# Hybrid encoder trunk on one core: the first two SSD heads prepared during the input projection, `x*dt` built per pair of heads, one 128-row spread matmul, and the MLA operands built during the last heads

## The reference

```python
def ssd_scan(x, dt, a, b_in, c_in):        # run forwards, and on the flipped sequence
    def step(state, inp):                  # chunks of 128 tokens
        xc, dtc, bc, cc = inp
        acum = jnp.cumsum(dtc * a, axis=1)
        diff = acum[:, :, None] - acum[:, None, :]
        decay = jnp.exp(jnp.where(causal, diff, -jnp.inf))
        cb = jnp.einsum('blgn,bsgn->blsg', cc, bc)
        scores = cb[..., None] * decay * dtc[:, None]
        y = jnp.einsum('blsge,bsgep->blgep', scores, xc)
        ...
def ssd_mla_mixer(h, w_in, ...):
    proj = jnp.einsum('bsd,df->bsf', h, w_in)
    z, xbc, dt_raw, q_a, kv_a = jnp.split(proj, [o1, o2, o3, o4], axis=-1)
    xbc = jax.nn.silu(dwconv_centred(xbc, conv_w, conv_b))
    ...                                    # xs, b_in, c_in from xbc; dt = softplus(...)
    y = y_fwd + y_bwd + xs * d_skip
    y = rmsnorm(y * silu(z), ssd_norm_w)
    o_mla = mla_attention(q_a, kv_a, ...)
    return jnp.einsum('bsf,fd->bsd', jnp.concatenate([y, o_mla], axis=-1), w_out)
```

## Time and profile before

| | us |
|---|---|
| median of 3 runs | 1456.57 (1453.92 to 1461.63) |
| profiled execution, its own time | 1456.77 |
| its span in the trace | 1454.9 |
| TensorE busy | 1386.8 (95% of the span) |
| VectorE busy | 826.2 (57%) |
| ScalarE busy | 644.8 (44%) |
| GpSimd busy | 634.0 (44%) |

### The profile page before, as it was taken

One profiled execution on the slowest core, in us unless ns is written; L12 is line 12 of the kernel. 1 busy time (PEld: TensorE's weight loads), 2 busy tenths in 40 slices (PEclk: granted clock), 3 DMA queues, 4 the chain that ended last, 5 costly groups with the idle time before them and its releaser, 6 DMA issues.

```text
span 1454.9 us, 16724 instructions
## 1 busy us (share of the span) xinstructions
PE 1386.8 (95%) x6722; PEld 1142.5 (79%) x6722; DVE 826.2 (57%) x980; ACT 644.8 (44%) x983; POOL 634.0 (44%) x291
## 2 busy tenths in 40 slices
PE   6999798898999999999999999997999999999997
PEld 6778565677889888888888977886798888888886
DVE  5656487564007999888100755345158998885003
ACT  4544375554234544444223465534444544443221
POOL 2345485103541455444555244422714554545550
PEclk9999899999999999999999999998999999999998
DMA  5222100112322232322333312211113323323331
GB/s 186 85 87 87 36 1 1 37 42 75 91 84 91 97 101 89 101 91 91 94 101 89 114 58 87 90 42 44 65 52 116 100 88 102 92 93 95 93 92 58
DMA packets 36685, 117.76 MB, mean 81 GB/s; under 512 B 3840, under 2 KB 8320, under 8 KB 36608
## 3 DMA queue, kind: packets, MB, share of 16 engines
q1 hardware_dynamic: 35888, 114.63, 25.0%
q10 hardware_dynamic: 720, 2.06, 0.4%
HBM read 114.58 MB, written 2.10 MB: 80 GB/s over the span
## 4 chain that ended last, share of the span: by engine, by line
PE 75%; DVE 7%; ACT 3%; issue 1%; POOL 0%; DVEq 0%; ACTq 0%
PE bank L312 22%; PE bank L314 22%; PE bank L313 22%; PE bank L1134 2%; PE bank L1267 1%; PE bank L1268 1%; DVE ebuf L1010 1%; DVE ebuf L1003 1%; PE bank L1290 1%; DVE xres L559 1%; PE bank L402 1%; ACT prob L1339 1%; PE bank L1471 0%; DVE xw_lo L578 0%; DVE m_ffn L552 0%
## 5 line engine op out<-in xcount | busy, mean ns | idle before, releaser
L295 POOL TENSOR_TENSOR wlo<-raw,whi 128x1024 fp32r<-128x1024 f32 (+2 forms) x216 | 529.2, 2464 | 704.5 <-ACT whi L289 704.4
L312 PE MATMUL bank<-xw_hi,whi 128*128 128x512 f32 (+1 forms) x1360 | 516.0, 379 | 16.0 <-DVE xw_lo L578 11.9
L314 PE MATMUL bank<-xw_hi,wlo 128*128 128x512 f32 (+1 forms) x1360 | 505.4, 372 | 0.0
L313 PE MATMUL bank<-xw_lo,whi 128*128 128x512 f32 (+1 forms) x1360 | 505.2, 371 | 0.0
L289 ACT ACTIVATE whi<-raw 128x1024 fp32r<-128x1024 f32 (+2 forms) x217 | 220.7, 1023 | 223.2 <-DMA raw<-in_fout 113.4
L312 PEld LDWEIGHTS bank<-xw_hi,whi 128*128 128x128 f32 x1360 | 259.4, 191 | 67.5 <-issue 17.9
L313 PEld LDWEIGHTS bank<-xw_lo,whi 128*128 128x128 f32 x1360 | 259.4, 191 | 47.3 <-issue 3.6
L314 PEld LDWEIGHTS bank<-xw_hi,wlo 128*128 128x128 f32 x1360 | 259.0, 190 | 45.1
L531 DVE RECIPROCAL small<-small 128x2 f32<-128x2 f32 (+1 forms) x12 | 2.0, 170 | 353.0 <-ACT small L468 337.4
L635 DVE SCALAR_TENSOR_TENSOR cbuf<-ubuf,par,cbuf 128x510 f32<-128x510 f32 x100 | 170.8, 1708 | 3.5
L631 DVE SCALAR_TENSOR_TENSOR cbuf<-ubuf,par,cbuf 128x510 f32<-128x510 f32 x100 | 149.9, 1499 | 0.6 <-ACT cbuf L665 0.6
(11 more groups left out here) (252 smaller groups left out, 1465.0 us busy)
## 6 DMA issues: line engine op xcount, KB each, us to landing
raw<-in_fin SPq DMA_DIRECT2D x88, 512.0 KB, 3.6
raw<-in_fout SPq DMA_DIRECT2D x32, 448.0 KB, 3.3
raw<-in_gin SPq DMA_DIRECT2D x25, 512.0 KB, 3.5
raw<-in_hin SPq DMA_DIRECT2D x24, 512.0 KB, 3.6
raw<-in_hout SPq DMA_DIRECT2D x16, 512.0 KB, 3.6
raw<-in_fout SPq DMA_DIRECT2D x16, 512.0 KB, 3.5
raw<-in_gout SPq DMA_DIRECT2D x8, 512.0 KB, 3.6
xres<-in_x SPq DMA_DIRECT2D x8, 256.0 KB, 7.6
```

Source lines behind the costliest of these rows:

```text
L295: engine.tensor_tensor(wlo[s][:, 0:n], raw[s][:, 0:n], whi[s][:, 0:n].bitcast(F32), ALU.subtract).then_inc(w_lo, 1)
L312: first = nc.tensor.matmul(out_ap, wh, ah, start=start, stop=False)
L313: nc.tensor.matmul(out_ap, wh, al, start=False, stop=False)
L314: return first, nc.tensor.matmul(out_ap, wl, ah, start=False, stop=stop)
```

## The change

It does four things. (a) `pe_x_turn` stands after z blocks 17, 18, 19 and 20; the last four z blocks use banks 6 and 7; and heads 0 and 1 are spread after block 21, their exponentials, minima and masks standing between the last z blocks on each engine. (b) `xdt` is cut by pair of heads (128x512 for one direction of one pair, all four token blocks), pairs 0 and 1 are made ahead of the masks of head 0, pairs 2 and 3 after the last z block, pairs 4 to 7 by GpSimd behind the masks of heads 2 to 9. (c) High and low part of the cumulated sum lie on 128 rows of one tile, `at_both`, the low part brought there by a DMA from ScalarE's queue, so one matmul replaces two. (d) The rounded MLA operands and the two matmuls on `mq` stand before the end of the heads.

```diff
@@ pe_hin
-            return bank[(4, 5)[j] if j < 2 else j % 2 if j >= 20 else (0, 1, 3)[(j - 2) % 3]]
+            return bank[(4, 5)[j] if j < 2 else 7 - j % 2 if j >= 20 else (0, 1, 3)[(j - 2) % 3]]
...
-                if j >= 20:
-                    pe.wait_ge(sem("hin_u"), (18, 19, 21, 22)[j - 20])
-                elif j >= 5:
+                if j == 21:
+                    pe.wait_ge(sem("cb_set"), 16)
+                elif j >= 22:
+                    pe.wait_ge(sem("hin_u"), j - 1)
+                elif 5 <= j < 20:
                     pe.wait_ge(sem("hin_u"), j - 2)
...
-            for t in range(Z0, 12):
-                if t == 11:
+                if 0 <= j - TURN0 < NBLK:
+                    pe_x_turn(pe, j - TURN0)
+                if j == 21:
                     pe.wait_ge(sem("hin_u"), 20)
                     pe_spread(pe, 0, True)
-                block(2 * t)
-                block(2 * t + 1)
-                pe_x_turn(pe, t - Z0)
+                    pe_spread(pe, 1, True)
@@ act_hin
+            act.wait_ge(sem("dt_dve"), 9)
+            act.dma_start(at_both[64:128, :].bitcast(F32), at_lo[:].bitcast(F32)).then_inc(sem("at_in"), 16)
             turns(act, SIDE, Z0, conv)
...
+            for j in range(2 * Z0, 24):
+                gate(j)
+                i = j - TURN0
+                if 0 <= i < NBLK:
+                    act.wait_ge(sem("xs_T"), 2 * i + 1)
+                    nc.scalar.activation(xtok[0][:, i * T:(i + 1) * T], bank[4][:],
+                                         ACT.Copy).then_inc(sem("xtok_act"), 1)
+                if j == 21:
+                    act_exps(act, 0)
+                    act_exps(act, 1)
@@ dve_hin
+                if j == 20:
+                    dve.wait_ge(sem("xtok_act"), NBLK)
+                    dve.wait_ge(sem("dt_dve"), 12)
+                    dve_xdt(dve, 0)
+                    dve_xdt(dve, 1)
+                if j == 21:
+                    dve_least(dve, 0)
+                    dve_least(dve, 1)
+                    dve_mask(dve, 0)
+                if j == 22:
+                    dve_mask(dve, 1)
@@ pool_hin
-            for at in range(BASE["hin"], BASE["hin"] + 23):
+            for at in range(BASE["hin"], BASE["hin"] + 22):
                 los(pool, at)
+            pool.wait_ge(sem("cb_mm"), NBLK)
+            pool.wait_ge(sem("xtok_act"), NBLK)
+            pool.wait_ge(sem("dt_dve"), 12)
+            pool_xdt(pool, 0, 1)
+            pool_xdt(pool, 1, 1)
+            pool_mask(pool, 0)
+            pool_mask(pool, 1)
+            los(pool, BASE["hin"] + 22)
@@ xdt by pair of heads
+        def xdt_part(engine, d, p):
+            f0 = d * NBLK * P
+            dt = dtt[:].rearrange("p (b n) -> p b n", b=NBLK)[:, :, d * 32 + 2 * p:d * 32 + 2 * p + 2]
+            return engine.tensor_tensor(
+                xdt[p][:, f0:f0 + NBLK * P].rearrange("p (b h e) -> p b h e", b=NBLK, e=HDIM),
+                xtok[p // 4][:].rearrange("p (b q h e) -> p b q h e", b=NBLK, q=4, h=2)[:, :, p % 4],
+                dt.unsqueeze(3).broadcast_to([P, NBLK, 2, HDIM]), ALU.mult)
@@ pool_ssd
+            pool.wait_ge(mm, BASE["hin"] + 24)
+            pool_xdt(pool, 2, 1)
+            pool_xdt(pool, 3, 1)
+            pool.wait_ge(sem("xtok_dve"), NBLK)
+            for n in range(2, HEADS):
+                pool_mask(pool, n)
+                if n < 10:
+                    pool_xdt(pool, 4 + (n - 2) // 2, n % 2)
@@ dve_ssd
+            dve_xdt(dve, 2)
+            dve_xdt(dve, 3)
+            dve.wait_ge(sem("xdt_pool"), 4)
+            dve.wait_ge(sem("xdt_dve"), 4)
...
+            for n in range(HEADS):
+                if n + 2 < HEADS:
+                    dve_least(dve, n + 2)
+                if n >= 2:
+                    dve_mask(dve, n)
+                if n % 2 and n >= 3:
+                    gated((n - 3) // 2)
+            dve_mla_low(dve)
             gated(KD - 1)
@@ act_ssd
-            for n in range(HEADS):
-                exps(n, n % 4, n < 4)
+            for n in range(2, HEADS):
+                act_exps(act, n)
                 if n % 2 and n >= 5:
                     square((n - 5) // 2)
+            act_mla_prep(act)
@@ pe_spread
-                pick = ident_r[:, 32 * d + n:32 * d + n + 1].to_broadcast([64, P])
-                nc.tensor.matmul(abank(v, d)[:], pick, at_hi[:],
-                                 start=True, stop=False)
-                nc.tensor.matmul(abank(v, d)[:], pick, at_lo[:],
-                                 start=False, stop=True).then_inc(sem("a_mm"), 1)
+                pick = ident_r[:, 32 * d + n:32 * d + n + 1].to_broadcast([P, P])
+                nc.tensor.matmul(abank(v, d)[:], pick, at_both[:], start=True, stop=True).then_inc(sem("a_mm"), 1)
@@ pe_ssd
-            pe.wait_ge(sem("hin_u"), 24)
-            pe_spread(pe, 1, True)
             pe_spread(pe, 2)
-            pe.wait_ge(sem("xdt_dve"), NBLK)
-            pe.wait_ge(sem("xdt_pool"), NBLK)
...
+                if n == HEADS - 1:
+                    pe_mla_prep(pe)
                 y(n)
```

More of the change, by code:

```diff
@@ L139, in build_program @@
         with ExitStack() as s:
-            xdt = sb("xdt", 2 * NBLK * D, F32, s)
+            xdt = [None, None] + [sb(f"xdt{p}", 2 * NBLK * P, F32, s) for p in range(2, PAIRS * 2)]
         with ExitStack() as s:
@@ L156, in build_program @@
             with ExitStack() as q:
+                with ExitStack() as q2:
+                    sb("xs_chunks", 8 * T, F32, q2)
+                    xdt[0:2] = [sb(f"xdt{p}", 2 * NBLK * P, F32, q2) for p in range(2)]
                 xbc = sb("xbc", 12 * T, F32, q)
@@ L1026, in gated @@
                 nc.vector.tensor_tensor(ck(zbuf, c), ck(zbuf, c), ck(xbc, c), ALU.mult).then_inc(sem("ssd_y"), 1)
-            def turn(n0, g, first=False, last=False):
-                for v in range(4):
-                    if v < 2 or not last:
-                        least(n0 + v + 2, (v + 2) % 4, first and v < 2)
-                    m(n0 + v, v, g)
-                    if (n0 + v) % 2 and n0 + v >= 3:
-                        gated((n0 + v - 3) // 2)
-            turn(0, 0, first=True)
-            turn(4, 0)
-            turn(8, 1)
-            turn(12, 1, last=True)
+            for n in range(HEADS):
[6 more added lines that the diff above has]
+            dve_mla_low(dve)
             gated(KD - 1)
@@ new lines, in act_exps @@
+        def act_exps(act, n):
+            v = n % 4
+            act.wait_ge(sem("a_mm"), 2 * n + 2)
+            if n == 0:
+                act.wait_ge(sem("dt_dve"), 12)
+            if n == 2:
+                act.wait_ge(sem("xdt_pool"), 4)
+                act.wait_ge(sem("xdt_dve"), 4)
+            if n >= 4:
+                act.wait_ge(sem("y_mm"), n - 3)
+            for r, s, a, b, l0 in TILES[0]:
+                nc.scalar.activation(ebuf[v][:, r * 384 + a:r * 384 + b],
+                                     abank(v, 0)[:, r * SEQ + l0:r * SEQ + l0 + b - a], ACT.Relu, scale=-1.0,
+                                     bias=acol[:, bass.ds((2 * r + s) * 64 + n, 1)]).then_inc(
+                                         sem("ssd_rel"), 1)
+            act.wait_ge(sem("ssd_rel"), 4 * n + 4)
+            nc.scalar.activation(ebuf[v][:, 0:768], ebuf[v][:, 0:768], ACT.Exp, scale=-1.0).then_inc(
+                sem("ssd_exp"), 1)
+            act.wait_ge(sem("ssd_min"), 4 * n + 4)
+            nc.scalar.activation(ebuf[v][:, 768:1536], ebuf[v][:, 768:1536], ACT.Exp).then_inc(
+                sem("ssd_exp"), 1)
@@ L1200, in dve_mla_low @@
                 dve.wait_ge(sem("mla_hi"), i + 1)
-                nc.vector.scalar_tensor_tensor(out=dst, in0=ck(mq, 1 + i), scalar=w, in1=src.bitcast(F32),
+                nc.vector.scalar_tensor_tensor(out=dst, in0=ck(mq, 1 + (i + 1) % 3), scalar=w, in1=src.bitcast(F32),
                                                op0=ALU.mult, op1=ALU.subtract).then_inc(sem("mla_lo"), 1)
         def pe_mla_prep(pe):
-            pe.wait_ge(sem("ssd_y"), 16)
-            nc.tensor.matmul(bank[4][:], con("seldup"), ck(mq, 0), start=True, stop=True)
@@ L1951, in _ @@
             act_ssd(act)
-            act_mla_prep(act)
             act_mla(act)
@@ L1969, in _ @@
             pool_hin(pool)
-            pool_xdt(pool)
             pool_ssd(pool)
```

185 lines of the change are left out of this document (75 added, 110 removed).

## The result

The changed kernel takes 1441.84 us (median of 4 runs, 1441.08 to 1442.44), before 1459.1 in the same comparison. The two medians differ by 17.3 us; the ratio of the measurement is 0.9892, with a 95% interval of 0.987 to 0.9914, which is 15.8 us less. The profiled execution took 1441.75 us with a span of 1439.6, which is 15.3 shorter than before. A later measurement of the same kernel gave 1444.45 (1440.91 to 1444.86; ratio 0.9903, interval 0.9882 to 0.9924). 1439.5 was forecast, with a range of 1435 to 1444: the first median lies inside it, the second 0.45 us outside.

The account below looks back on a forecast made before the run. TensorE, busy 95% of the span, was taken as the bound, with time to win at waits or half clock. Terms -15.0 - 0.9 + 2.1 + 2.0 - 5.4 = -17.2 gave 1439.5 us, range 1435 to 1444.

Parts of the forecast that it names:

- The start of the heads: Heads 0 and 1 prepared under the last z blocks, xdt by pair: gain 15.0 us, between 13.5 and 16.5.
- One spread matmul: Two matmuls per head fewer; only the last two spreads of the heads give something: gain 0.9 us, bounds 0 and 4.7.
- The price in mid-heads: From head 4 on GpSimd has six xdt pieces left instead of four: loss 2.1 us, bounds 0 and 3.5.
- The end of the heads: Matmuls on mq before y of head 15 lose 2.0 us; first queries directly behind y of head 15 gain 5.4.
- close; if it is late, up to 0.7 us: VectorE's six operations beside the first queries, 4.2 us, against 4.3 us until TensorE needs the first: nothing new late.
- everything behind is the same work: After the heads, the same work follows on a chain that starts earlier, the rest of the trace shifted by 17 us.
- Heads 0 and 1 not ready: Rival: ScalarE 5 us late with head 1, TensorE waits over 3 us, the clock falls: 1447.3 us; 8%.
- slower: Rival: TensorE at the lower clock throughout the heads, 2 us lost per head, 1468 us with all 14; 3%.
- a wait of 1.65 us was followed by full clock: Argument against a lower clock in the heads; the longest wait found in the new order was 1.6 us.
- The spread saving counts in full: Rival: TensorE at 3.38 us per head sets the pace, 3.8 more from spreads, no loss of 2.1: 1433.6 us; 10%.
- mid-heads pay more: Rival: VectorE's 12 masks from head 4 on each wait 0.6 us more for GpSimd, costing 7 us: 1446.5; 16%.

Follow-up runs that it names:

- e3_heads_late: The changed kernel with spreads, exponentials, minima and masks of heads 0 and 1 behind the last z block instead of block 21: 1450.52 us.
- e7_fill_wait: The changed kernel with five idle matmuls in TensorE's 3.04 us wait between the first two MLA scores: 1440.71 us.
- e2_mla_end: The changed kernel with the two matmuls on mq, ScalarE's copies and VectorE's remainders behind head 15 again: 1446.55 us.
- e5_no_late_xdt: The changed kernel without GpSimd's eight pieces of xdt for pairs 4 to 7, so it does not compute the encoder: 1438.88 us.
- e6_early_xdt45: The changed kernel with GpSimd's four xdt pieces of pairs 4 and 5 made right behind those of pairs 2 and 3: 1439.58 us.
- e8_mask_first: The changed kernel with VectorE's mask of head n ahead of its least of head n+2 instead of behind it: 1443.97 us.

## Why the prediction was right, and where its terms were off

**The start of the heads.** Forecast 15.0 us at `least` of head 6, measured 14.4 (197.70 to 183.26). Every station came within 0.7 us: last z block 168.4 (168.7 forecast), y of head 0 169.38 (169.8), head 2 on ScalarE 171.77 (171.8), y of head 2 178.43 (178.6). `e3_heads_late` shows that 8.4 us of the 13.8 at y of head 2 go when heads 0 and 1 lose their place under the last z blocks, `xdt` of pairs 2 and 3 being held up with them. The rest comes from `xdt` and the turns; it was not taken apart further. The drain of about 1.38 us that the Trainium skill ("ScalarE: Activation LUTs", What ACT_TABLE_LOAD costs) adds to a switch did not appear: Relu ends at 173.12, the load takes 173.14 to 174.42, and Exp begins at 174.44.

**One spread matmul.** Forecast gain 0.9. Right in kind: 0.75 us over six heads, where 2.8 was the full saving, and nothing measurable in the time of the kernel before, though its trace shows 2.7.

**The price in mid-heads.** Forecast loss 2.1, to be set against the 0.9, so +1.2 for both. Before, y of head 13 ends here:

```profile
238.25 1.12 PE L1153 MATMUL bank<-rstd,ones 128*128 128x512 f32 x2
```

From `least` of head 6 to this point the kernel before needs 40.6 us (197.70 to 238.25). The first profile of the changed kernel needs 40.0 (183.26 to 223.24), which is -0.6 for both terms. Its second profile needs 42.9 (184.05 to 226.90), and that of `e7_fill_wait` 42.8: +2.3, of which 1.7 is y of head 10 at half clock. So the forecast of +1.2 lies between the profiles, and the first, on which the comparison with the forecast rests, is the favourable one. `e2_mla_end`, whose heads are the same up to head 13, goes like the second (182.88 to 225.72, 42.8).

The mechanism was half right. VectorE's masks took 1.57 us in the first profile and 1.80 in the second (1.51 before). GpSimd's instructions grew a little too (masks from 2.06 to 2.21 us, `xdt` from 1.58 to 1.72, in the stretches of the earlier trace rows and of 182 to 222), and with two more pieces its idle time went from 6.6 us in 31.4 to none. What the forecast left out is that ScalarE must wait for GpSimd's additions, which costs most at head 10. GpSimd's timeline in mid-heads:

```profile
186.71 1.82 POOL L987 TENSOR_TENSOR ebuf<-ebuf,cbm 128x768 f32<-128x768 f32 x1
188.49 1.76 POOL L973 TENSOR_TENSOR xdt<-xtok,dtt 128x512 f32<-128x512 f32 x1
190.21 2.26 POOL L987 TENSOR_TENSOR ebuf<-ebuf,cbm 128x768 f32<-128x768 f32 x1
```

and VectorE's beside it:

```profile
187.06 2.28 DVE L1041 TENSOR_TENSOR ebuf<-ebuf,cbm 128x768 f32<-128x768 f32 x1
```

VectorE's mask begins at 187.06 under GpSimd's, ends 0.8 us after it, and only then does GpSimd's `xdt` get on: 1.76 us instead of the 1.04 that it takes without such a mask beside it (178.25). This is how two engines would alternate on an exclusive lock held for a whole instruction (the Trainium skill, "SBUF — State Buffer", Who interferes with whom). The trace agrees, at 0.72 us for this turn; no run separates the lock from other causes. From 178 to 209 neither GpSimd nor VectorE has a gap, at 3.73 us a head (heads 2 to 8). The chain that ended last goes through GpSimd there, and `e5_no_late_xdt` shows that time is won when GpSimd's work goes.

**The end of the heads.** Forecast -5.4 and +2.0, so -3.4; measured from the end of y of head 13 to the first queries 8.86 us instead of 11.6: -2.8 (8.46 and -3.2 in the second profile). Behind it, "close; if it is late, up to 0.7 us": the copy that TensorE waits for was late, by 0.65 (9.73 from the queries to the scores, 9.08 before), because VectorE's two half additions took 2.07 us instead of 1.40, beside GpSimd's addition of squares.

**What the sum left out.** In the first profile the gain was 17.8 us against 17.2 forecast at the first queries, 17.1 at the first scores, 15.7 at the end of MLA (353.86 to 338.20) and 15.3 at the end of the span. The step that did not hold is "everything behind is the same work": the second scores ran at half clock for 6 us instead of 3, which took 1.45 us back. The second profile keeps full clock there and loses at head 10 instead; it has gained 14.5 us at the first queries and 12.2 at the end of its span. So part of the closeness to 1439.5 is luck: terms missed in both directions cancel in the first profile, and the second measurement falls just outside the range.

**The rivals.** "Heads 0 and 1 not ready" and "slower" did not happen; the clock was 1.00 in 170 to 190. But the argument against a falling clock ("a wait of 1.65 us was followed by full clock") was too weak: the clock fell at heads 9 or 10, behind waits of 1.75 and 1.83 us, where the prediction found none longer than 1.6. In `e3_heads_late` it stayed up behind the same two waits (1.75 and 1.82), so their length alone does not decide it. "The spread saving counts in full" needed 3.38 us a head and "mid-heads pay more" about 4.4; heads 2 to 8 took 3.73.

## What to carry to other kernels

A preparation chain of two or three engines that stands between two dense stretches of TensorE is worth moving under the first of them, even at the price of two more table loads: here that place and the earlier `xdt` that goes with it gave 8.4 of 15 us. When TensorE is made cheaper in a stretch where VectorE and GpSimd are near full, little comes of it (0.75 of 2.8 us); look first at whether GpSimd has an idle microsecond left. Taking work off the fuller of two such engines pays only until the other is full: eight pieces of about 1.7 us off GpSimd gave 2.1 to 4.6 us. And follow what the late engine releases: here one addition, made late, stopped ScalarE for 4 us. Compare a forecast with more than one profile of the same kernel; two of this one differ by 2.5 us in the heads alone.

## What the runs showed of the hardware

- TensorE's clock fell behind waits of 1.75 and 1.83 us (heads 9 and 10), and 1.5 us after a wait of 3.63 us had ended, in the midst of dense matmuls. The same waits were followed by the lower level in one execution and by the upper one in another: 1.75 us at head 9 (first and second profile), 3.04 us at the scores (the same two), 1.82 us at head 10 in `e3_heads_late`.
- Executions of the changed kernel differ by up to 4 us (1440.91 to 1444.86 in one measurement). Of the executions of `e6_early_xdt45` the three shorter ones have a mean clock of 0.987 to 0.988 and the three longer ones 0.983. That the clock makes the whole difference is not shown.
- GpSimd's 128x512 product took 1.04 us (178.25, beside VectorE's `least`) and 1.76 us beside VectorE's mask; VectorE's 128x768 mask took 0.95 at its shortest and up to 2.57 beside GpSimd's (`e8_mask_first`).
- A switch of ScalarE's table cost 1.28 us in all three places in and around the first heads (159.36, 165.62, 173.14), with at most 0.03 us on either side.
